# Attention stage of a hybrid encoder layer: the order of three engines' queues written as tables of turns

## The chip, the cores and the metric

The kernel runs on one core of a Trainium2 chip. The metric is the time of one execution on the device, in microseconds. TensorE (PE), VectorE (DVE), ScalarE (ACT), GpSimd (POOL) and SyncE (SP, which issues the transfers) each work through a queue of their own in program order, and wait for each other by semaphores.

## The reference, cut to what matters

One layer with two groups of heads over a prompt of 4096 frames, and a small batch of new frames for eight streams. Mixer A (8 heads) is attention over a window of about 192 keys with a sink per head. Mixer B (8 heads) is attention over 256 chosen keys per query: an indexer scores all admissible keys, the 256 best are kept. For the attention of mixer B the reference reads, cut:

```python
r = relu(einsum('bqhe,ble->bqhl', qi, ki_all))
score = where(adm, einsum('bqhl,bqh->bql', r, wi), -inf)
_, idx = top_k(score, topk)                      # 256 of up to 4096
s = einsum('bqhgd,bqkhd->bqhgk', q, k_all[bi, idx]) * HEAD_DIM ** -0.5
w = softmax(where(valid, s + bias, -inf))
o = einsum('bqhgk,bqkhd->bqhgd', w, v_all[bi, idx])
y = concatenate([oa * silu(ga), ob * silu(gb)]) @ w_out
```

## The kernel before

The program has three stages, one after the other: projections with the indexer and the choice of keys, attention of the prompt (`stage_two`), and the output projection with all of the small batch. The change is in the attention stage alone.

The prompt is cut into 32 tiles of 128 queries. A tile has six jobs: two of mixer A (four heads each, up to 256 keys) and four of mixer B (two heads each, all keys up to the tile's own end, with a mask that is minus a large number where a key was not chosen). A job runs in steps: two for mixer A, one per 512 keys for mixer B, so the number of steps of a tile grows from 8 to 36, and there are 704.

A job's work, engine by engine:

- TensorE `score`: a score unit of up to 512 keys for two heads (L1565, L1576), into one of two PSUM slots.
- VectorE `use`: adds mask or bias, writes the row to SBUF and takes its maximum in parts (L1811 to L1824 for mixer A, L1837 for B); `finish_top` joins the parts (L1850).
- ScalarE `exponential`: in place over the row, 1024 keys at a time (L1673), and the sinks (L1659).
- TensorE `turn`: a step's transposes of the row, four blocks for each of two heads, into one PSUM bank per head (L1592).
- ScalarE (L1771) copies the first head's bank to SBUF, VectorE (L1948) the second head's. The transposes of the next step into a bank wait for its copy.
- TensorE `apply`: the value products of a step from the copies (L1621). The copies are double, so a copy also waits for the products of two steps before.
- The gate: VectorE scales it (L1858 to L1869), TensorE transposes it (`turn_gate`, L1631), ScalarE copies it (L1681), VectorE multiplies (`mix`, L1878).

Two rows of choices, those of tiles 30 and 31, are not ready from the first stage. ScalarE searches their thresholds beside its other work (`late_search`, L1706 and L1688, some 160 turns for each row), and VectorE makes the mask from the result (`late_close`, L1886 to L1929; one of its instructions is a scan over the whole row, L1915).

The order on each engine is written by loops over jobs and steps. On TensorE:

```python
turn(n, g)
for kind, m, j in PLACED[n, g]:
    score(m, j)          # or turn_gate
if last is not None:
    apply(*last)
last = (n, g)
```

So after the transposes of a step come the score units placed at it, and then the value products of the step before. VectorE copies a step, then uses the units placed there; ScalarE copies, then does the exponentials that `PLAN` gives to the step, gate copies, and the late turns that `LATE_ACT` spreads evenly (tiles 3 to 18 and 20 to 28). `LATE_DVE` puts the closing of the late rows into tiles 19 and 29.

Of the kernel before, what the change touches and what calls it, by code (L numbers as in the profile page):

```python
# [128 lines left out]
TESTS = 32  # L129
# [117 lines left out]
""")  # L247

# [1050 lines left out]
LATE_SPANS = {1: ((3, 27, 28),), 2: ((3, 18, 19), (20, 28, 29))}[len(LATE_TILES)]  # L1299


def wide_steps(first, last):

    return [(n, g) for n in range(6 * first, 6 * last + 6) if n % 6 >= 2 for g in range(n_steps(n))]
# [5 lines left out]


LATE_ACT = {_s: 0 for _s in STEP_AT}
LATE_DVE = {_s: 0 for _s in STEP_AT}
for _a, (_first, _last, _close) in zip(LATE_TILES, LATE_SPANS):
    _steps = [(n, g) for n, g in wide_steps(_first, _last) if n % 6 != 5 or g < n_steps(n) - 1]
    _many = TESTS * (len(quarters(_a)) + 1) + 1
    for _i in range(_many):
        LATE_ACT[_steps[_i * len(_steps) // _many]] += 1
    _steps, _many = wide_steps(_close, _close), 2 + 5 * len(quarters(_a)) + 1
    for _i in range(_many):  # L1320
        LATE_DVE[_steps[_i * len(_steps) // _many]] += 1
# [12 lines left out]
def stage_two(nc, rel_bias, sink_a, eye, qk_t, gates, values, chosen, late, ramp, mixed, a_k_prompt, a_v_prompt):  # L1334
    with ExitStack() as ctx:
# [89 lines left out]
        def _(sp):  # L1425
# [121 lines left out]
        def _(pe):  # L1547
# [86 lines left out]
            score(0, 0)  # L1634
            score(1, 0)
            last = None
            for n in range(N_JOBS):
                for g in range(n_steps(n)):
                    turn(n, g)
                    for kind, m, j in PLACED[n, g]:  # L1640
                        if kind == "score":
                            score(m, j)
                        else:
                            turn_gate(m, j)
                    if last is not None:
                        apply(*last)
                    last = (n, g)
            apply(*last)
            turn_gate(TILES - 1, 1)

        @block.scalar
        def _(act):
# [37 lines left out]
            def late_search():  # L1690
# [7 lines left out]
                for i, a in enumerate(LATE_TILES):  # L1698
# [37 lines left out]
                    yield  # L1736
# [23 lines left out]
            late_work = late_search()  # L1760

            for x in PLAN["first"]:
                exponential(*x)
            for n in range(N_JOBS):
                for g in range(n_steps(n)):
                    at = STEP_AT[n, g]
# [5 lines left out]
                    for x in PLAN[n, g]:  # L1772
                        exponential(*x)
                    for kind, m, j in PLACED[n, g]:
                        if kind == "gate":
                            copy_gate(m, j)
                    for _ in range(LATE_ACT[n, g]):
                        next(late_work, None)
            for _ in late_work:
                pass  # L1780
            copy_gate(TILES - 1, 1)

        @block.vector
        def _(dve):
# [17 lines left out]
            def use(n, j):  # L1802
# [5 lines left out]
                if k < 2:  # L1808
                    keys = a_keys(t)
# [14 lines left out]
                    dve.tensor_scalar(top_a[:, k, :], part_a[:, :], -1.0, None, ALU.mult).then_inc(s_top, 1)  # L1824
                    return
                parts = [(i, p) for i, p in enumerate(biased_parts(n)) if c_in(p[0], *score_units(n)[j])]
                for h in range(2):
# [11 lines left out]
                ins.then_inc(s_used, 1)  # L1839
# [4 lines left out]
            def finish_top(n):  # L1844

                k, many = n % 6, len(biased_parts(n))
                dve.wait_ge(s_used, max(UNIT["score", n, j] for j in range(len(score_units(n)))) + 1)
# [32 lines left out]
            def late_close():  # L1880

                over, left, value, low, step, more = (l_pick[:, i:i + 1] for i in range(6))
                for i, a in enumerate(LATE_TILES):
# [31 lines left out]
                    m = tick(dve.tensor_tensor_scan(row, tie, tie, 0.0, ALU.add, ALU.max))  # L1915
                    dve.wait_ge(s_dve, m)
# [6 lines left out]
                    for q, (c, n) in enumerate(parts):  # L1923
                        dve.wait_ge(s_dve, tick.n)
                        tick(dve.scalar_tensor_tensor(late_mask[:, c:c + n], late_tie[:, c:c + n], BIG, late_mask[:, c:c + n], ALU.mult, ALU.add))
                        if q < len(parts) - 1:
                            yield
# [4 lines left out]
            late_work = late_close()  # L1932

            use(0, 0)
            use(1, 0)
            for n in range(N_JOBS):
                t, k = divmod(n, 6)
                if k == 2:
                    scale_gate(t, 0)
                if k == 5:  # L1940
                    scale_gate(t, 1)
                for g in range(n_steps(n)):
                    at = STEP_AT[n, g]
# [5 lines left out]
                    for kind, m, j in PLACED[n, g]:  # L1949
                        if kind == "score":  # L1950
                            use(m, j)
                        else:
                            mix(m, j)
                    for _ in range(LATE_DVE[n, g]):
                        next(late_work, None)
                for m in range(n, min(n + 5, N_JOBS)):
                    if m % 6 >= 2 and job_whose_row(m) == n:
                        finish_top(m)
            mix(TILES - 1, 1)
# [577 lines left out]
```

## Time and profile before

| | us |
|---|---|
| median of three runs | 4878.95 |
| lowest and highest | 4876.77, 4880.1 |
| the profiled execution | 4880.94 |
| its span in the trace | 4879.1 |
| PE busy in the span | 4278.2 (88%) |
| DVE, ACT busy | 3502.0 (72%), 3431.7 (70%) |

Busy shares are means over three stages. The attention stage is the stretch from 2265 us (the first transposes) to 4277 us of the span. Matmuls are pipelined, so the start of one record to the start of the next says more of its cost than its length does.

### The profile page before, as it was taken

Reading aid. Unit: us, or ns where it says so; the run is one execution under the profiler, and the core shown is the slowest. Engines: PE = TensorE matmul, PEld = TensorE weight load, DVE = VectorE, ACT = ScalarE, POOL = GpSimd, SP = SyncE. Lnnn points to the kernel's source line nnn. Section 1 sums busy time; section 2 is a strip of 40 time slices with the busy share of each in tenths; the row PEclk is TensorE's granted clock in tenths of the full one; section 3 lists DMA queues with packets and bytes.
Section 4 is the critical chain, followed back from the end, with each engine's and each line's share of the span. In section 5 each row is a group of like instructions: output and inputs, shape, how many; then the busy total and the mean of one; then the engine's idle time right before and its main releaser. Section 6 shows DMA issues by size and latency. Waiting matters only on the chain. (4 is left out here: it accounts for less than half of the span.)

```text
span 4879.1 us, 78367 instructions
## 1 busy us (share of the span) xinstructions
PE 4278.2 (88%) x26505; PEld 2688.7 (55%) x26505; DVE 3502.0 (72%) x6644; ACT 3431.7 (70%) x6887; POOL 1611.0 (33%) x1358
## 2 busy tenths in 40 slices
PE   7898988778887796763899999999999999989999
PEld 3454444434444343332667777777777777744544
DVE  2478889999999898997777777877677778624111
ACT  1699999999999797932788888688888775510100
POOL 1466667767676777790110000000000000000000
PEclk9999988888898897886999999999999999999999
DMA  6221111111111110014211111010101000055332
GB/s 151 75 73 35 50 40 38 37 36 38 45 48 43 44 43 30 33 70 130 73 55 55 42 41 42 27 57 28 41 24 40 32 25 25 10 162 135 100 101 98
DMA packets 201975, 276.98 MB, mean 57 GB/s; under 512 B 50496, under 2 KB 134176, under 8 KB 201056
## 3 DMA queue, kind: packets, MB, share of 16 engines
q1 hardware_dynamic: 198624, 271.81, 17.7%
q8 instruction: 220, 3.60, 0.3%
q14 instruction: 171, 1.40, 0.1%
q10 hardware_dynamic: 2960, 0.17, 0.0%
HBM read 156.73 MB, written 114.16 MB: 56 GB/s over the span
## 5 line engine op out<-in xcount | busy, mean ns | idle before, releaser
L603 PE MATMUL bank<-w,x 128*128 128x512 f32 (+1 forms) x2848 | 1220.4, 584 | 69.2 <-ACT ring L704 56.3
L1043 DVE TENSOR_SCALAR_CACHE_REDUCE ties<-score,cand 128x512 int8<-128x512 f32 (+13 forms) x448 | 1110.6, 2479 | 82.0 <-POOL score L920 66.2
L603 PEld LDWEIGHTS bank<-w,x 128*128 128x128 f32 x2848 | 551.9, 198 | 645.6 <-issue 525.6
L808 ACT ACTIVATE act_junk<-score,a_cand,a_sign 128x384 int8<-128x384 f32 (+13 forms) x420 | 879.5, 2094 | 14.0
L1837 DVE CUSTOM_DVE_ANT_0 row<-bank,mask 128x512 f32<-128x512 f32 (+3 forms) x1024 | 622.5, 639 | 180.8 <-PE bank L1576 180.1
L1543 POOL TENSOR_TENSOR near_bias<-table,mask 128x2048 f32<-128x2048 f32 (+1 forms) x32 | 129.5, 4048 | 1765.0 <-DVE part L1837 1749.5
L1771 ACT ACTIVATE pT<-bank 128x512 f32<-128x512 f32 (+2 forms) x704 | 368.3, 523 | 427.1 <-PE bank L1592 425.0
L1673 ACT ACTIVATE row<-row,top 128x1024 f32<-128x1024 f32 (+7 forms) x640 | 632.8, 990 | 4.0 <-DVE top L1850 4.0
L1576 PE MATMUL bank<-kT,qb 64*128 64x256 f32 (+1 forms) x4352 | 608.0, 396 | 9.3 <-DVE part L1837 5.9
L1592 PE MATMUL bank<-ident,row 128*128 128x128 f32 x4224 | 593.8, 281 | 25.4 <-DVE pT L1948 19.0
L619 PE MATMUL bank<-kiT,qi 128*128 128x512 f32 (+3 forms) x1136 | 405.3, 493 | 233.8 <-ACT relu L739 233.4
L1948 DVE COPY pT<-bank 128x512 f32<-128x512 f32 (+2 forms) x704 | 425.2, 604 | 255.5 <-PE bank L1592 253.4
L1621 PE MATMUL bank<-pT,v 128*64 128x128 f32 x8448 | 590.3, 280 | 0.0
L915 POOL TENSOR_TENSOR score<-score,relu 128x512 f32<-128x512 f32 (+3 forms) x426 | 553.5, 1299 | 33.4
L1621 PEld LDWEIGHTS bank<-pT,v 128*64 128x64 f32 x8448 | 450.9, 137 | 170.8 <-issue 163.4
L912 POOL TENSOR_TENSOR relu<-relu,weight 128x512 f32<-128x512 f32 (+3 forms) x426 | 500.0, 1174 | 90.7 <-ACT relu L739 90.3
L1592 PEld LDWEIGHTS bank<-ident,row 128*128 128x128 f32 x4224 | 452.8, 141 | 131.2 <-issue 97.5
L2293 PE MATMUL bank<-wo,mix_in 128*128 128x512 f32 x1024 | 451.1, 599 | 0.0
L1576 PEld LDWEIGHTS bank<-kT,qb 64*128 64x128 f32 x4352 | 379.3, 187 | 125.3 <-issue 71.8
L619 PEld LDWEIGHTS bank<-kiT,qi 128*128 128x128 f32 x1136 | 238.0, 225 | 373.5 <-ACT relu L739 291.9
L739 ACT ACTIVATE relu<-bank 128x512 f32<-128x512 f32 (+3 forms) x568 | 292.5, 558 | 119.5 <-POOL score L915 95.0
L2293 PEld LDWEIGHTS bank<-wo,mix_in 128*128 128x128 f32 x1024 | 194.2, 192 | 234.5 <-issue 234.1
(255 smaller groups left out, 4852.5 us busy)
## 6 DMA issues: line engine op xcount, KB each, us to landing
qk_t<-ring SPq DMA_DIRECT2D x66, 256.0 KB, 2.0
gates<-ring SPq DMA_DIRECT2D x66, 256.0 KB, 2.0
gate<-gates SPq DMA_DIRECT2D x33, 512.0 KB, 3.4
out<-x_in SPq DMA_DIRECT2D x33, 512.0 KB, 2.9
x<-in_x_prompt SPq DMA_DIRECT2D x32, 512.0 KB, 3.6
mixed<-mixT SPq DMA_DIRECT2D x64, 256.0 KB, 2.0
mix_in<-mixed SPq DMA_DIRECT2D x32, 512.0 KB, 4.2
x_in<-in_x_prompt SPq DMA_DIRECT2D x32, 512.0 KB, 3.9
```

Source lines behind the costliest of these rows:

```text
L603: ins = pe.matmul(p_bank[n % 2][:, 0:n1 - n0], held[:, c * P:(c + 1) * P], w[:, c, n0:n1], start=(c == 0), stop=(c == KC - 1))
L619: ins = pe.matmul(s_bank[at % 4][:, 0:n], qi[:, part, h * P:(h + 1) * P], kiT[:, c:c + n], start=(part == 0), stop=(part == 1))
L808: tick(act.activation(junk, row, ACT.Sign, bias=c, scale=back, accum_out=a_sum[:, :]))
L912: k = tick(pool.tensor_tensor(r, r, weighs, ALU.mult))
L915: pool.tensor_tensor(to, to, r, ALU.add).then_inc(s_pa, 1)
L1043: n = tick(dve.tensor_scalar(ties[:, 0:width], row, c.bitcast(F32), 0.0, ALU.is_ge, ALU.add, accum_out=counts[:, i:i + 1]))
L1576: ins = pe.matmul(s[:, h * STEP + c0:h * STEP + c0 + m], qb[t % 2][half, g, :], kT[half, c + c0:c + c0 + m], start=True, stop=True)
L1592: ins = pe.transpose(t_bank[h][:, b * P:(b + 1) * P], held, ident[:, :])
L1621: ins = pe.matmul(oT[0 if k < 2 else 1][half * HD:(half + 1) * HD, col:col + P], value, pT[h][at % 2][:, b * P:(b + 1) * P], start=first, ...
L1673: act.activation(at, at, ACT.Exp, bias=bias, accum_out=out).then_inc(s_exp, 1)
L1837: ins = dve.tensor_tensor_reduce(row[k % 2][:, h, c0:c0 + w0], s[:, h * STEP + c0 - c:h * STEP + c0 - c + w0], more, 1.0, PAD, ALU.add, AL ...
L2293: ins = pe.matmul(y_bank[k % 2], held, w[:, c, i * STEP:(i + 1) * STEP], start=(c == 0), stop=(c == KC - 1))
```

## The change

Each of the three engines' orders becomes a table, as a string of letters with counts; a generator per kind of work yields after each item, and `take_turns`, which is there already for the first stage, takes the next item of the kind that the table names. Each kind keeps its own order. TensorE has transposes of one head (`t`), score units and gates (`u`) and value products of a step (`v`); ScalarE has copies (`p`), exponentials (`e`), gate copies (`g`) and late turns (`l`); VectorE has copies (`p`), joined maxima (`t`), pieces of units and mixes (`u`), gate scalings (`k`) and late closing (`l`). The even spreads of late work are gone. A score unit's pieces on VectorE are separate turns; since the table may now put them before work that the loops had put first, `use` and `finish_top` wait for the maximum before and for the transposes that read the old row. SP loads the second late row at tile 19 instead of 20. `PLACED` and `PLAN` still give the sequence within a kind.

```diff
+PE_TURNS_2 = in_turn("""
+u2 t6 u2 v2 t2 v2 t3 v t v u5 t3 u t v t u t v t u t2 v2 t2 v t3 v t2 v2 u4 t2 u t u t v t v t u t u t v t2 v t v t2
...
+ACT_TURNS_2 = in_turn("""
+e3 p e4 p e9 p2 e3 p e p g e4 p2 e4 p e4 p e2 g e5 p e2 p e3 p2 l6 g l2 e3 p e l p l e3 p e6 p g e6 p e2 p e3 p l g l
...
+DVE_TURNS_2 = in_turn("""
+u2 p4 u3 t u t p2 k u3 t u2 t u p u2 p t k u p u2 p u t u p4 k u3 t u2 t u p u k p u3 t u p u2 p u3 p t k p2 u3 p u3 t
...
-                if t in [close + 1 for _, _, close in LATE_SPANS[:-1]]:
-                    load_late([close + 1 for _, _, close in LATE_SPANS].index(t) + 1)
+                if t in LATE_LOADS:
+                    load_late(LATE_LOADS.index(t) + 1)
...
                         ins = pe.transpose(t_bank[h][:, b * P:(b + 1) * P], held, ident[:, :])
                     ins.then_inc(s_t0 if h == 0 else s_t1, 1)
+                    yield
...
+            def applies():
+                for n, g in STEP_AT:
+                    apply(n, g)
+                    yield
+
+            take_turns(PE_TURNS_2, t=turns(), u=units(), v=applies())
...
+            take_turns(ACT_TURNS_2, p=copies(), e=exponentials(), g=gate_copies(), l=late_search())
...
                 if k < 2:
+                    dve.wait_ge(s_top, TOP_AT[n])
+                    if t:
+                        dve.wait_ge(s_t1, STEP_AT[n - 6, n_steps(n - 6) - 1] + 1)
...
+                if t:
+                    before = job_whose_row(n)
+                    dve.wait_ge(s_top, TOP_AT[before] + 1)
+                    dve.wait_ge(s_t1, STEP_AT[before, min(j, n_steps(before) - 1)] + 1)
...
-                ins.then_inc(s_used, 1)
+                        if h == 1 and (i, (c0, w0, near)) == parts[-1]:
+                            ins.then_inc(s_used, 1)
+                        yield
...
+            take_turns(DVE_TURNS_2, p=copies(), t=tops(), u=uses(), k=gates_scaled(), l=late_close())
```

`take_turns`, unchanged:

```python
def take_turns(order, **work):
    for kind, many in order:
        for _ in range(many):
            next(work[kind])
```

## Rows read from the trace of the kernel before

**Rows 1.** Windows: stretch, us, busy of PE, PEld, DVE, ACT, POOL (instructions), clock.

```profile
2264.99:2831.61 566.62, 524.64 (x5008) 385.33 (x5008) 420.84 (x1276) 459.52 (x1219) 61.27 (x15) 0.97 0.21 65
2831.61:3257.46 425.85, 405.06 (x4043) 307.06 (x4041) 322.38 (x873) 332.61 (x771) 24.90 (x6) 0.98 0.13 42
3257.46:4277.38 1019.92, 1006.34 (x10242) 771.04 (x10240) 726.97 (x1929) 759.11 (x1634) 41.23 (x10) 1.00 0.09 29
```

**Rows 2.** Who waited for whom in the attention stage: us in total, times, longest us.

```profile
PE bank L1592 <- DVE pT L1948: 32.6, 31, 8.2
...
PE bank L1592 <- ACT pT L1771: 26.5, 73, 1.8
...
PE bank L1592 <- ACT row_a L1673: 13.1, 1, 13.1
```

**Rows 3.** Timeline of TensorE in tile 19: start us, us, line, operation, records.

```profile
3100.19 0.66 PE L1592 MATMUL bank<-ident,row_a 128*128 128x128 f32 x4 [0.26 <-ACT pT L1771]
3100.77 0.66 PE L1621 MATMUL bank<-pT,va 128*64 128x128 f32 x8
...
3103.67 0.66 PE L1621 MATMUL bank<-pT,va 128*64 128x128 f32 x8
3104.26 1.09 PE L1592 MATMUL bank<-ident,row 128*128 128x128 f32 x8
3105.29 1.13 PE L1576 MATMUL bank<-kT,qb 64*128 64x256 f32 x8
3106.35 1.09 PE L1621 MATMUL bank<-pT,v 128*64 128x128 f32 x16
3107.38 1.09 PE L1592 MATMUL bank<-ident,row 128*128 128x128 f32 x8
...
3113.60 1.09 PE L1592 MATMUL bank<-ident,row 128*128 128x128 f32 x8
3114.53 0.60 PE L1631 MATMUL bank<-ident,scaled 128*128 128x128 f32 x4
```

**Rows 4.** Timeline of TensorE in tile 22: two score units in a row.

```profile
3408.16 1.13 PE L1565 MATMUL bank<-ka,qa 64*128 64x256 f32 x8
3409.13 1.03 PE L1576 MATMUL bank<-kT,qb 64*128 64x256 f32 x8
3410.09 1.09 PE L1621 MATMUL bank<-pT,v 128*64 128x128 f32 x16
```

**Rows 5.** Timeline of all engines, tile 25: transposes and their two copies.

```profile
3600.82 1.09 PE L1592 MATMUL bank<-ident,row 128*128 128x128 f32 x8
...
3601.52 0.60 ACT L1771 ACTIVATE pT<-bank 128x512 f32<-128x512 f32 x1 [0.87 <-PE bank L1592]
...
3601.95 0.69 DVE L1948 COPY pT<-bank 128x512 f32<-128x512 f32 x1 [0.59 <-PE bank L1592]
```

**Rows 6.** Timeline of all engines, tile 23: a copy, and transposes waiting for it.

```profile
3421.68 0.38 ACT L1771 ACTIVATE pT<-bank 128x256 f32<-128x256 f32 x1
...
3422.12 0.66 PE L1592 MATMUL bank<-ident,row_a 128*128 128x128 f32 x4 [0.26 <-ACT pT L1771]
```

**Rows 7.** Windows for lines L1706 and L1688 alone: stretch, us, ACT busy (instructions).

```profile
2264.99:4277.38 2012.39, 334.56 (x512) 0.99 0.13 42
...
2264.99:4277.38 2012.39, 70.01 (x294) 0.99 0.13 42
```

**Rows 8.** View by windows, tiles 20 to 24.

```profile
3178.50:3589.14 410.64, 404.24 (x4095) 307.95 (x4094) 292.89 (x819) 336.71 (x746) 20.42 (x5) 1.00 0.12 39
```

**Rows 9.** Groups by form on DVE: count, busy us, mean ns, idle before.

```profile
L1837 DVE DVE_READ_ACCUMULATOR2_ANT part<- 128x1 f32 x1336 | 110.8, 83 | 0.0
```

**Rows 10.** View by windows of tile 19; waits of TensorE in tile 19, then in tile 29.

```profile
3094.77:3178.50 83.73, 73.23 (x718) 55.99 (x716) 77.13 (x174) 44.46 (x105) 4.46 (x1) 0.94 0.10 31
...
PE bank L1592 <- DVE pT L1948: 9.8, 3, 8.2
...
PE bank L1592 <- DVE pT L1948: 6.1, 3, 5.4
```

More of the change, by code:

```diff
@@ new lines @@
+t v2 u2 t3 v u t2 u v2 u t4 u t2 v2 u2 t2 v2 t2 u t2 u t2 v2 u t2 u t2 v2 u2 t2 v u t2 v u t2 v u t2 u t2 v2 u t2 u
+t2 v2 u2 t2 v2 u2 t4 v2 u t2 u t2 v u t2 v t2 v2 t4 u t2 v2 u2 t2 v2 t2 u t2 v2 u2 t2 u t2 u t2 v2 u2 t2 v2 t2 u t2
+v2 u2 t4 v u t2 u v2 u t4 v u t2 u2 t v2 u t4 v u t2 u t v2 u2 t2 v2 t2 u t2 v u2 t2 v u t2 u t2 v2 u2 t2 v2 t2 u t2
+v2 t4 v t2 v u t2 u t2 v2 u2 t2 v2 t2 u t2 v u2 t2 u t2 v2 u2 t2 v2 u t4 v u t2 u t2 v2 u2 t2 v2 t2 u t2 v u t2 u2 t
+v2 u t4 v2 u2 t4 v2 u2 t2 u t2 u t v2 u2 t2 v2 u2 t4 v u t2 v2 u2 t2 u t2 v t2 v2 t4 u t2 v2 u2 t2 v2 t2 u t2 v2 u2
@@ new lines @@
+t4 u t2 v2 u2 t2 v2 t2 u t2 v2 u2 t4 v u2 t2 u t2 v2 u2 t2 v2 u t4 v u t2 u t2 v2 u t2 v2 t4 v2 t4 v2 t4 v2 t2 u t2
+v2 t4 v2 t4 v2 t4 v2 t4 v2
+""")
+ACT_TURNS_2 = in_turn("""
+e3 p e4 p e9 p2 e3 p e p g e4 p2 e4 p e4 p e2 g e5 p e2 p e3 p2 l6 g l2 e3 p e l p l e3 p e6 p g e6 p e2 p e3 p l g l
+p l2 e3 p e l p e7 p e3 l p g e3 p e4 p e3 p l g l p l2 e4 p l p e5 p e5 l p l e3 p e g e3 p e3 p g l p l2 p l p e2 p
+e2 l p l2 p l p l e9 p e p g e5 p e4 p e g l p l p l3 p e p e l e p e p l3 p e2 p e7 p e p l g l e6 p e2 p e p e g p
@@ new lines @@
+e3 p2 e2 p4 e3 p e3 p e4 p e4 p e4 p e4 p3 e g e p e2 p e p e2 p e p5 g p3 e2 p e2 p e2 p e2 p5 e2 p e3 p e3 p3 e2 p3
+e2 p e4 p e4 p e4 p e4 p e4 p2 g p e p e2 p e p e p e p e2 p5 g p2 e3 p e2 p e2 p e p4 e2 p e2 p e2 p e2 p2 e2 p3 e2
+p e2 p e6 p e2 p e2 p e5 p e3 p2 g p e p e2 p e p e2 p e p e p4 g p3 e3 p e3 p e2 p5 e p e p e2 p e p e2 p e p2 g p9
+""")
+DVE_TURNS_2 = in_turn("""
+u2 p4 u3 t u t p2 k u3 t u2 t u p u2 p t k u p u2 p t u p4 k u3 t u2 t u p u k p u3 t u p u2 p u3 p t k p2 u3 p u3 t
@@ L247 @@
+u2 l u p u l2 p u2 p u2 l4 p u2 p u2 l3 p u p u3 l t l2 p u2 p u2 p u2 k p u2 p u p u4 p u p u5 t p u2 p u2 p u2 p u3
+p u2 p u2 p u2 p u4 k p t u p4 u2 p u2 p u4 p2 u2 p u2 p u3 p u4 t p u4 p2 u2 p u2 p u2 p u2 p u2 p u4 t u2 p2 u2 p
+u2 p u2 k u p u2 p u2 p u5 p u t p u2 p u2 p u2 p u3 p u2 p u2 p u2 p u4 k t u p5 u2 p u4 p2 u2 p u2 p u2 p u2 p u5 t
+p u4 p2 u2 p u2 p u2 p u4 p2 u4 t p6 k p10 u
 """)
@@ L1298 @@
 QUARTER = 1024
-LATE_SPANS = {1: ((3, 27, 28),), 2: ((3, 18, 19), (20, 28, 29))}[len(LATE_TILES)]
-def wide_steps(first, last):
-    return [(n, g) for n in range(6 * first, 6 * last + 6) if n % 6 >= 2 for g in range(n_steps(n))]
+LATE_LOADS = (19,)
 def quarters(a):
     return [(c, min(QUARTER, (a + 1) * P - c)) for c in range(0, (a + 1) * P, QUARTER)]
[L1312 to L1321, printed above, removed]
 def exps_of_job(n):
@@ L1632, in turn_gate, with turns, units @@
                 ins.then_inc(s_unit, 1)
[L1634 to L1649, printed above, removed]
+            def turns():
+                for n, g in STEP_AT:
+                    yield from turn(n, g)
+            def units():
+                for kind, n, j in UNIT:
+                    if kind == "score":
+                        score(n, j)
+                    else:
+                        turn_gate(n, j)
+                    yield
+            def applies():
+                for n, g in STEP_AT:
+                    apply(n, g)
+                    yield
+            take_turns(PE_TURNS_2, t=turns(), u=units(), v=applies())
         @block.scalar
@@ L1758, in late_search, with copies @@
                     yield
[L1760 to L1766, printed above, removed]
+            def copies():
+                for (n, g), at in STEP_AT.items():
                     act.wait_ge(s_t0, at + 1)
@@ L1771, in _, with exponentials, gate_copies @@
                     act.activation(pT[0][at % 2][:, 0:cols], t_bank[0][:, 0:cols], ACT.Copy).then_inc(s_c0, 1)
-                    for x in PLAN[n, g]:
+                    yield
+            def exponentials():
+                for s in ["first"] + list(STEP_AT):
+                    for x in PLAN[s]:
                         exponential(*x)
[L1774 to L1781, printed above, removed]
+                        yield
+            def gate_copies():
+                for kind, t, b in UNIT:
+                    if kind == "gate":
+                        copy_gate(t, b)
+                        yield
+            take_turns(ACT_TURNS_2, p=copies(), e=exponentials(), g=gate_copies(), l=late_search())
         @block.vector
@@ L1915, in late_close @@
                     m = tick(dve.tensor_tensor_scan(row, tie, tie, 0.0, ALU.add, ALU.max))
+                    yield
                     dve.wait_ge(s_dve, m)
@@ L1930, in late_close, with copies @@
                     yield
[L1932 to L1943, printed above, removed]
+            def copies():
+                for (n, g), at in STEP_AT.items():
                     dve.wait_ge(s_t1, at + 1)
@@ L1948, in _, with tops, uses, gates_scaled @@
                     dve.tensor_copy(pT[1][at % 2][:, 0:cols], t_bank[1][:, 0:cols]).then_inc(s_c1, 1)
[L1949 to L1959, printed above, removed]
+                    yield
+            def tops():
+                for n in TOP_AT:
+                    if n % 6 >= 2:
+                        finish_top(n)
+                        yield
+            def uses():
+                for kind, n, j in UNIT:
+                    if kind == "score":
+                        yield from use(n, j)
+                    else:
+                        mix(n, j)
+                        yield
+            def gates_scaled():
+                for t in range(TILES):
+                    for b in range(2):
+                        scale_gate(t, b)
+                        yield
+            take_turns(DVE_TURNS_2, p=copies(), t=tops(), u=uses(), k=gates_scaled(), l=late_close())
 NEW = BATCHES * DEC
```

81 lines of the change are left out of this document (78 added, 3 removed).

## The prediction

> **What bounds the kernel now.** I read the profile by stretches of the attention stage, cut where the first transposes of tiles 0, 15 and 21 start; it takes 2012 us of the 4879 [rows 1]. Tensor is busy in 525 of 567, 405 of 426 and 1006 of 1020 us, so the later the tile the more it alone sets the pace; its idle time is 42.0 + 20.8 + 13.6 = 76.4 us. Scalar has 107, 93 and 261 us free, vector 146, 103 and 293. Next the waits of tensor [rows 2]: 32.6 us for vector's copies of transposed blocks, 26.5 us for scalar's, and 13.1 us once at the start, for the first exponentials. That is all that an order can remove as idle time.
>
> Busy time is not all work. In the timeline of tensor [rows 3] a step in the middle of a tile goes round without a gap in 3.12 us: 8 transposes 1.03 (3104.26 to 3105.29), one score unit 1.06, 16 value records 1.03. The 4 transposes of a mixer-A step take 0.58 to the next start and the 8 of a mixer-B step 1.03, so one costs 0.11, and each visit to the transposes has a fee of 1.03 - 0.88, some 0.14. Value products: 0.59 for two blocks (3103.67), 1.03 for four, so 0.22 a block and a fee of 0.15. Where 8 transposes are followed by the gate's transposes the next start comes after 0.93 (3113.60 to 3114.53): the part of the fee that is paid on leaving is 0.09, on entering 0.05. Two score units in a row [rows 4] take 1.93 (3408.16 to 3410.09), so the second adds 0.87 and the fee of a visit is 0.19. With the order of the loop, tensor makes 705 visits to transposes (the gate's among them), 563 to scores, 703 to value products: 98.7 + 107.0 + 105.5 = 311 us of fees. A reordering can thus change tensor's busy time, not only its waits.
>
> **What the change does, part by part.** No matrix, vector or scalar operation is added or dropped; the orders on tensor, scalar and vector are replaced by tables. I counted the tables against the loops.
>
> *Fewer visits.* The new tensor table has 626 visits to transposes, 491 to scores, 431 to value products. Saved: 79 x 0.14 + 72 x 0.19 + 272 x 0.15 = 11.1 + 13.7 + 40.8 = 65.5 us; by stretch 14.7, 12.6, 38.2. The trace before has no two value products in a row that show a merged visit, nor scores followed by transposes; a merged value visit saves between 0 and 0.15. I take 0.15, since the merged score units and the transposes before the gate's both save the whole fee. With 0 the savings would be 24.8 us.
>
> The Trainium skill, TensorEngine Tiling (Array Packing), Key Properties, says that changing the tiling mode, not just the tile, drains TensorE. The three kinds here have shapes 128*128, 64*128 and 128*64, and the rows agree in that transposes after transposes pay no fee. By it merged value products save all of their 40.8 us, as taken.
>
> *Transposes with nothing between.* In the loop at least one value product or unit stands between the transposes of a step and those of the next. In the table 215 steps have nothing there. The transposes of the next step write the same bank, so they wait for the copy. From [rows 5]: transposes start at 3600.82, scalar's copy of the first head starts 0.70 later and takes 0.60, and tensor resumes 0.06 after a copy's end (3421.68 + 0.38 to 3422.12, [rows 6]): 1.36. Tensor comes to the next transposes after 0.05 + 8 x 0.11 = 0.93. So it stands 0.43 us at each place where both heads come right before; there are 114 (30, 21 and 63 by stretch): 49.0 us. The second head follows vector's copy, ready 1.13 + 0.69 + 0.06 = 1.88 after the start, against 1.36 + 0.44: 0.08 more in the 81 of them where it follows at once, 6.5 us. In the other 101 the first head of the step had gone earlier; in 42 of these the second head follows directly and waits for vector's copy, 1.39 - 0.93 = 0.46: 19.3 us. Together 74.9 us (19.7, 14.4 and 40.8), with copies that start at once. If the copies come late it is more; where another engine holds tensor up anyway it is less, down to half.
>
> *Waits of the old order.* Of the 76.4 us, 13.1 belong to the start and stay. The two long waits for vector, 8.2 us in tile 19 and 5.4 in tile 29 [rows 10], stand where the loop puts vector's closing of a late row, whose scan is one instruction in both kernels; the table moves the first close to tiles 14 and 15 and leaves the scan of the second in tile 29, so I let both stay. Of the other 49.7 us, most stand before transposes of mixer A, where the loop has one value product alone between two steps; the table has 45 such places instead of 110 (the bare ones are charged above). None to all may come back; I take half, 24.9 us.
>
> *Late search on scalar.* It was spread evenly over tiles 3 to 18 and 20 to 28. The table packs it: 160 turns in tiles 0 to 14 (101 before), 22 in tiles 15 to 20 (77), 138 after (144). A turn is (334.6 + 70.0) / 322 = 1.26 us [rows 7]. In the first stretch scalar goes from 459.5 to 534 of 567 us; with the 13.1 at the start 547 is its floor, and my forecast for the stretch is 566.6 - 14.7 + 19.7 - 14.5 = 557. In tiles 20 to 24 there are 142 turns for 83: 336.7 + 59 x 1.26 = 411 us, in a time that is now 410.6 [rows 8]. So those tiles cannot become faster, whatever tensor saves. Tensor's own account there is near even too, so I add nothing; the bound above is the rival.
>
> *Vector's units in pieces, more waits.* A unit's pieces become single turns, so a copy can go between two of them. New waits on maxima and on the second head's transposes come to some 1,400; each stands in front of its unit, and copies queue behind it. No row shows a wait's own price; between nothing and the shortest vector row, 0.083 us [rows 9], that is 0 to 116 us, beside vector's 542 free ones [rows 1]. I take nothing; without that cover it would be slower by as much as lies on the path. The load of the second late row is asked for one tile earlier on SP; its wait for the first mask is over by then (closed in tile 15), so the loads queued behind it are not held.
>
> **Sum.** -65.5 + 74.9 - 24.9 = -15.5 us on the profiled execution's 4880.94, that is 4865.4. That execution is 2.0 above the median of the runs, 4878.95, so I predict 4863. The last stage follows attention on tensor, so what is gained there counts in full.
>
> **The rivals.**
> 1. *Scalar is crowded, slower.* The place is tiles 0 to 14 and 20 to 24, 302 turns of late search. One that stands ahead of a copy that tensor is about to need costs up to its 1.26 us. For it: scalar has no free time left in tiles 20 to 24. Against: turns are placed where the tables leave scalar nothing else. With one turn in eight, 38 x 1.26 = 48 us, and the result is 4911. It decides from about one in fifteen: 25 us, which ends above the median.
> 2. *Much faster.* The fees go as worked out, half of the bare waits fall together with waits that are there anyway (37 us), and all 49.7 us come back: -65.5 + 37.5 - 49.7 = -78, 4801. For it: 29 of the old waits are in the first stretch, where mixer A has much of the work. Against: in tiles 21 to 31, where tensor has 98.7% already, savings (38.2) and bare waits (40.8) cancel.
> 3. *No change.* Fees and bare waits cancel, and what of the old waits comes back is spent on late copies: within 10 us of 4879. This is the case in which the change doesn't do what it says: the tables give tensor's priorities, but it runs its queue in order and waits where the table has nothing to put in.
> 4. *The clock.* After the 8.2 us wait the granted clock of tile 19 is 0.94 [rows 10], so 83.7 x 0.06 = 5 us of full clock were lost; in tiles 20 to 24 it is 1.00. If many short stops did the same in ten tiles, 50 us: 4913. The stops here are 0.43 us, a stop of 0.26 at 3422.12 [rows 6] lies in tiles at 1.00, and so do the other short ones there, so I give it little. The Trainium skill, TensorE: Matmul & The Clock Gate, A second HAM failure mode, describes such falls from frequent short idling between groups of matmuls; the trace of before does not show one.
>
> **How the numbers follow.** Forecast 0.37 (4845 to 4872), much faster 0.18, no change 0.18, scalar crowded 0.24, clock 0.03. A difference under 0.2%, 10 us, is about what a measurement of this kernel can't tell from none: faster means under 4869, slower over 4889. The forecast lies nearly all under 4869, so faster 0.52, same 0.20 (no change and the forecast's upper edge), slower 0.28 (the two slow rivals and a little of no change). The range goes to 4815 (most of rival 2's way, its bottom left out) and 4908 (most of rival 1): 0.08 and 0.12 stay outside. The forecast's own range is 4845 to 4872.
>
> **What the profile after would show.** Value products, scores and transposes with a lower busy sum, some 60 us less of tensor's busy time in the attention stage, against more idle time: waits before transposes for scalar's and vector's copies near 100 us where they were 59, in many short pieces of 0.4. Scalar over 95% busy in tiles 20 to 24, and around 60% after tile 25. Tensor's waits in tile 19 gone and 8 us in tile 15. I am wrong on the fees if busy time stays; on the bare waits if idle time stays near 76; and if tensor waits for scalar's exponentials or copies by 0.5 to 1.3 us at a time in tiles 20 to 24, it is rival 1.

## The result, and the profile after

After: 4890.61 us, median of 12 runs (4886.7 to 4897.69), against 4878.93 for the kernel before in the same rounds. The ratio is 1.0025 (95% interval 1.0016 to 1.0033): slower by 0.25%, where I forecast 4863 and faster. The time lies inside the range, the direction was wrong. One run of a later experiment (84 places filled) took 5427.57 us at a granted clock of 0.78 instead of 0.93 and is left out of its median.

The loss is in the attention stage: 2025.9 us instead of 2012.4 in the profiled executions. What lies outside it, where the two kernels are alike, was 6.2 us shorter there, so the two spans differ by 7.3 us only. By windows (stretch, us, busy of PE, PEld, DVE, ACT, POOL, clock), the three stretches of [rows 1], then tile 19 [rows 10] and tiles 20 to 24 [rows 8]:

```profile
2262.20:2831.73 569.53, 514.46 (x4993) 388.06 (x4994) 425.62 (x1294) 526.88 (x1371) 61.31 (x15) 0.97 0.20 65
2831.73:3251.72 419.99, 400.35 (x4071) 310.75 (x4069) 305.17 (x860) 275.54 (x646) 24.54 (x6) 0.99 0.13 42
3251.72:4288.10 1036.38, 989.03 (x10230) 776.94 (x10228) 703.12 (x1924) 748.32 (x1607) 41.74 (x10) 1.00 0.09 29
3098.30:3168.60 70.30, 69.22 (x714) 54.13 (x713) 49.51 (x144) 43.31 (x98) 4.10 (x1) 1.00 0.19 67
3168.60:3588.91 420.31, 400.30 (x4118) 311.64 (x4116) 281.78 (x817) 403.54 (x890) 20.44 (x5) 1.00 0.10 33
```

TensorE is busy for 1903.8 us instead of 1936.0, yet idle for 122.1 instead of 76.4. The stretches came out 2.9 slower, 5.8 faster and 16.5 slower. Tile 19 got 13.4 faster, since the closing of a late row left it (it now stands in tiles 14 and 15, which got 15.5 slower together); tiles 20 to 24 got 9.7 slower, with ACT busy for 96%.

The waits of TensorE in the attention stage (us in total, times, longest), answering to [rows 2]:

```profile
PE bank L1678 <- ACT pT L1854: 44.9, 90, 1.6
PE bank L1678 <- DVE pT L2037: 40.2, 48, 6.2
PE bank L1678 <- ACT row_a L1762: 16.6, 7, 13.4
PE bank L1708 <- DVE pT L2037: 10.5, 9, 6.9
...
PE bank L1708 <- ACT pT L1854: 4.4, 12, 0.6
```

L1678 is the transposes, L1708 the value products. Transposes wait for copies for 85.1 us where it was 59.1. New is that value products wait too, 14.9 us.

What joining visits gives shows in TensorE's timeline of tile 25:

```profile
3645.47 1.09 PE L1678 MATMUL bank<-ident,row 128*128 128x128 f32 x8
3646.49 1.97 PE L1708 MATMUL bank<-pT,v 128*64 128x128 f32 x32
3648.39 2.00 PE L1662 MATMUL bank<-kT,qb 64*128 64x256 f32 x16
3650.32 1.09 PE L1678 MATMUL bank<-ident,row 128*128 128x128 f32 x8
```

Two steps' value products take 1.90 (3646.49 to 3648.39) where two visits took 2 x 1.03 [rows 3]; two units take 1.93. The fees are gone as worked out.

A place where the transposes of a step follow directly on those of the step before is called bare from here on; there are 215. TensorE can go on there only when the bank that it is about to write again has been copied. A bare place whose copy starts at once, which is called a prompt copy below (tile 31; a bracket gives the idle time before and what ended it):

```profile
4274.73 1.09 PE L1678 MATMUL bank<-ident,row 128*128 128x128 f32 x8
4275.43 0.60 ACT L1854 ACTIVATE pT<-bank 128x512 f32<-128x512 f32 x1 [2.49 <-PE bank L1678]
...
4276.08 1.19 PE L1678 MATMUL bank<-ident,row 128*128 128x128 f32 x8 [0.25 <-ACT pT L1854]
```

From start to start 1.35 us, forecast 1.36. And one whose copy does not (tile 22):

```profile
3346.22 1.09 PE L1678 MATMUL bank<-ident,row 128*128 128x128 f32 x8
...
3347.58 0.39 ACT L1777 ACTIVATE l_cand<-l_sign,l_cand,l_step 128x1 f32<-128x1 f32 x1
3347.87 0.58 ACT L1854 ACTIVATE pT<-bank 128x512 f32<-128x512 f32 x1
...
3348.50 1.09 PE L1678 MATMUL bank<-ident,row 128*128 128x128 f32 x8 [1.20 <-ACT pT L1854]
```

Here ACT is in a late turn until 3347.87, and such a place costs 2.28 us.

To split the difference I went through TensorE's records item by item. An item's price is the least time from its start to the next one's start that occurs for the same kinds of neighbours; what an item takes beyond it is a wait. Price and waits are counted from the first score units on, some 15 us ahead of tile 0, so their sum is larger than the attention stage.

| kernel | visits: transposes, units, products | price | waits | attention |
|---|---|---|---|---|
| before | 705, 563, 703 | 1892 | 134 | 2012 |
| after | 626, 491, 431 | 1840 | 199 | 2026 |
| 115 bare places made in before | 590, 563, 703 | 1886 | 228 | 2100 |
| 178 joined units in before | 705, 385, 703 | 1856 | 167 | 2009 |
| 141 chosen pairs in before | 705, 422, 596 | 1849 | 137 | 1972 |
| after, 84 bare places filled | 709, 491, 513 | 1856 | 180 | 2024 |
| after, 177 products moved | 776, 491, 571 | 1873 | 205 | 2065 |
| own tables | 723, 427, 599 | 1852 | 94 | 1933 |

So the tables save 51 us of fees and add 65 us of waits. The split depends on how finely neighbours are told apart: finer and coarser classes give 45 to 60 us saved and 58 to 74 added, always some 14 us apart.

### The profile page after: what moved, and what is told of

It is laid out like the page before. It is cut to its first block and busy times, and to the rows that moved or that the text cites. A ratio compares the mean times of both kernels' runs of the same rounds, so it can differ in the third digit from the quotient of the medians.

```text
span 4886.4 us, 79007 instructions
## 1 busy us (share of the span) xinstructions
PE 4242.2 (87%) x26505; PEld 2698.8 (55%) x26505; DVE 3465.8 (71%) x6644; ACT 3431.1 (70%) x6887; POOL 1612.1 (33%) x1358
## 5 line engine op out<-in xcount | busy, mean ns | idle before, releaser
L1678 PE MATMUL bank<-ident,row 128*128 128x128 f32 x4224 | 604.9, 282 | 78.6 <-ACT pT L1854 41.6
L1933 DVE CUSTOM_DVE_ANT_0 row<-bank,mask 128x512 f32<-128x512 f32 (+3 forms) x1024 | 620.3, 635 | 37.8 <-PE bank L1662 15.9
L1662 PE MATMUL bank<-kT,qb 64*128 64x256 f32 (+1 forms) x4352 | 584.0, 394 | 10.0 <-DVE mixT L1977 7.8
L1678 PEld LDWEIGHTS bank<-ident,row 128*128 128x128 f32 x4224 | 454.7, 141 | 247.5 <-issue 123.4
L1708 PE MATMUL bank<-pT,v 128*64 128x128 f32 x8448 | 550.6, 279 | 3.4 <-DVE pT L2037 1.3
L1708 PEld LDWEIGHTS bank<-pT,v 128*64 128x64 f32 x8448 | 458.0, 137 | 74.8 <-issue 69.4
```

The costliest lines, as they stand in the source:

```text
L1662: ins = pe.matmul(s[:, h * STEP + c0:h * STEP + c0 + m], qb[t % 2][half, g, :], kT[half, c + c0:c + c0 + m], start=True, stop=True)
L1708: ins = pe.matmul(oT[0 if k < 2 else 1][half * HD:(half + 1) * HD, col:col + P], value, pT[h][at % 2][:, b * P:(b + 1) * P], start=first, ...
L1933: ins = dve.tensor_tensor_reduce(row[k % 2][:, h, c0:c0 + w0], s[:, h * STEP + c0 - c:h * STEP + c0 - c + w0], more, 1.0, PAD, ALU.add, AL ...
```

## The experiments

Theory 1 was that the fees are real and that bare places and late copies ate them; the rivals were that ACT and DVE set the pace, the added DVE waits, and the late work.

**Bare places filled (177 products moved).** In the changed kernel:

```diff
+def filled(order):
+    out, halves = [], 0
+    for kind in [kind for kind, many in order for _ in range(many)]:
+        if kind == "t":
+            halves += 1
+            if halves % 2 and halves > 1 and out[-1] == "t":
+                k = len(out) - 2
+                k -= out[k] == "t"
+                while k > 0 and out[k] not in "tv":
+                    k -= 1
+                if out[k] == "v":
+                    out.append(out.pop(k))
+        out.append(kind)
+    return [(kind, 1) for kind in out]
...
-            take_turns(PE_TURNS_2, t=turns(), u=units(), v=applies())
+            take_turns(filled(PE_TURNS_2), t=turns(), u=units(), v=applies())
```

> The changed kernel with one thing altered: wherever transposes of a step directly follow transposes of the step before, the nearest value product that stands ahead of them is moved in between; that fills 177 places and leaves 38. ACT and DVE keep the changed tables. Theory 1 (bare places cost more than forecast, since copies are late): the 97 us that TensorE waits in bare places after the change falls by about four fifths (-80), some 140 value-product visits come back at 0.15 (+21), 150 transposes' visits at about 0.04 net (+5): about -54 us, near 4836. Theory 2 (ACT and DVE set the pace, waits of TensorE only move): no gain, the fees come on top, 4890 to 4920. Theory 3 (the added waits on DVE made it slower): as theory 2, within 4890 to 4916.

Measured 4931.52, 1.0105 of before (1.0091 to 1.0119), 41 us above the changed kernel. Theory 1 failed outright. The rule moved 177 products, but it took some of them out of a place that it had filled just before: 157 places end up filled and 58 stay bare, not 38. The price rose by 33 us and the waits did not fall. In 34 places the wait was now for a copy that itself waited for the value product just put in front (copies are double): 27.5 us. Units waited more for their slots (2.0 and 7.8 us in the changed kernel):

```profile
PE bank L1679 <- DVE part L1950: 14.2, 27, 2.5
PE bank L1679 <- DVE mixT L1994: 10.6, 11, 6.0
```

**Filled only where that cannot happen (84).** The same function, but only between two whole steps and only with the product of the step before:

```diff
-            if halves % 2 and halves > 1 and out[-1] == "t":
-                k = len(out) - 2
-                k -= out[k] == "t"
+            if halves % 2 and halves > 1 and out[-2:] == ["t", "t"]:
+                k = len(out) - 3
...
-                if out[k] == "v":
+                if out[k] == "v" and halves // 2 - out[:k].count("v") == 2:
```

> The changed kernel, filled in 84 places only: those where the step's two transposes stand together and the value product moved in between is that of the step before (which the waiting copy does not itself wait for; in the run with 177 filled places 31 waits were for a copy that waited for the very product moved in between). Theory 1 (a bare place costs its copy's whole time, more than the visits it saves): 84 x 0.38 to 0.5 us of waits go (-32 to -42), 84 value-product and transposes' visits come at 0.15 + 0.09 (+20): -12 to -22 us, 4869 to 4878. Theory 2 (a bare place costs about what it saves, the loss is elsewhere): within 6 us of 4890.

Measured 4889.92, 1.0021 of before (1.0012 to 1.003): the changed kernel's time to within a microsecond. Theory 2 holds. In 29 of these places the copy had been prompt; the 0.36 us wait went and a fee of 0.15 to 0.2 came. In most of the others the wait stayed: of 55 places where ScalarE was still at something else when the transposes ended, 44 wait in this kernel too, and 29.9 of 41.8 us are left. The place of tile 22 shown above, in this kernel:

```profile
3342.73 0.93 PE L1694 MATMUL bank<-ident,row 128*128 128x128 f32 x7
3343.59 1.09 PE L1724 MATMUL bank<-pT,v 128*64 128x128 f32 x16
...
3345.00 0.57 ACT L1870 ACTIVATE pT<-bank 128x512 f32<-128x512 f32 x1
...
3345.62 1.09 PE L1694 MATMUL bank<-ident,row 128*128 128x128 f32 x8 [0.94 <-ACT pT L1870]
```

TensorE now does 1.03 us of work in the gap and still waits 0.94. The work is not new: the product stood ahead of the transposes, so these now start earlier against ACT's queue. ACT's copy starts 2.44 us after them (the first starts at 3342.56, just outside the view), where it was 1.65. At such places the next transposes come when ACT's queue reaches the copy, and not sooner for work moved on TensorE.

**Bare places in the loops.**

```diff
+                two = u != s and u[0] == s[0] and s[0] % 6 >= 2 and s[0] >= 6 * 8 and plain(s) and plain(u)
+                seen += two
+                if two and seen % 2 == 0:
+                    turn(*s)
+                    turn(*u)
+                    place(s)
+                    apply(*last)
+                    place(u)
+                    apply(*s)
```

> The kernel before, where in 89 of 178 pairs of steps of a wide job (tiles 8 to 31, every second pair) the second step's transposes are moved up directly behind the first's: 89 bare places are made and 89 visits to transposes saved, nothing else. Theory 1: each costs the wait for a copy, 0.4 to 0.6 us in the changed kernel's bare places, less about 0.04 net of a visit: +32 to +50 us, 4911 to 4929. Theory 2 (TensorE's waits are slack of other engines, so a wait made here is given back at the next one): less than +10 us.

Measured 4963.15, 1.0171 (1.0157 to 1.0185): +83.9 us. The rule made 115 pairs, not 89 (after a pair that is passed over, its second step may begin the next), so 0.73 us each, above theory 1's price. Of 80 us of waits in these places, 91 that wait for a prompt copy on ACT have 33 (0.36 each); the 16 behind DVE's gate scalings and the late closing have 18, and 19 behind late turns on ACT have 19. The price fell by only 5.7 us, 0.05 per merged visit to the transposes. Theory 2 is out here: in the loops' order nothing gives such a wait back.

**Score units joined.**

```diff
+                if two:
+                    turn(*s)
+                    place(s)
+                    place(u)
+                    apply(*last)
+                    turn(*u)
+                    apply(*s)
```

> The kernel before, where in 178 pairs of steps of a wide job (tiles 8 to 31) the second step's score unit is moved up directly behind the first's, ahead of the value product: transposes, two units, value product, transposes, value product. That saves 178 visits to score units and makes no bare place. Theory 1 (a visit's fee is real and gained in full where no wait comes in its place): 178 x 0.19 = -34 us, near 4845. Theory 2 (other engines set the pace): 0 to +10, since TensorE then only waits longer for copies and units' banks.

Measured 4874.01, 0.9988 (0.9979 to 0.9997). The price fell by 35.5 us, 0.20 for each of 178 visits: theory 1's fee, which made 34. The waits rose by 32.4. Two kinds grew, those for units' slots (5.9 us in 9 waits before) and those for ScalarE's copies (26.5 in 73):

```profile
PE bank L1576 <- DVE part L1854: 14.9, 38, 1.6
PE bank L1592 <- ACT pT L1788: 40.0, 93, 2.3
```

The second unit of a pair comes while DVE still uses the slot. The time, 5 us below before, lies between the theories and near theory 2 (0 to +10), while the fee is theory 1's.

**Pairs chosen.** Units joined in 141 pairs (all in tiles 8 to 31), the value products too in 107 of them, in the places where by the traces' durations neither a copy nor a slot comes late.

```diff
+                turn(*s)
+                place(s)
+                if i in SPLIT or i in WHOLE:
+                    u = steps[i + 1]
+                    place(u)
+                    if i in WHOLE:
+                        turn(*u)
+                    apply(*last)
+                    if i in SPLIT:
+                        turn(*u)
+                    apply(*s)
```

> The kernel before with 141 pairs of steps of a wide job joined (tiles 5 to 31), chosen so that by the durations in the traces neither a copy nor a unit's bank comes late: both score units stand together in all of them (141 x 0.20 = -28 us by the prices of the run with 178 pairs), and in 107 the two value products as well (107 x 0.15 = -16 us). DVE and ACT keep the loops of before. Theory 1 (a saved visit is gained where no copy or bank comes late in its place): -44 us, near 4835. Theory 2 (ACT and DVE set the pace, so most is given back as waits, as in the run with 178 pairs, which kept 5 of 35): -6 us, near 4873.

Measured 4835.57, 0.9911 (0.9897 to 0.9924): -42 us, theory 1, and faster than both kernels. The stretches:

```profile
2262.98:2824.84 561.86, 519.22 (x5008) 387.25 (x5008) 418.22 (x1276) 457.93 (x1219) 61.29 (x15) 0.97 0.21 65
2824.84:3243.03 418.19, 396.27 (x4042) 309.44 (x4041) 318.95 (x873) 329.85 (x771) 24.88 (x6) 0.99 0.13 42
3243.03:4235.19 992.16, 977.38 (x10242) 780.19 (x10240) 713.49 (x1930) 750.38 (x1634) 41.22 (x10) 1.00 0.09 30
```

27.8 us come from tiles 21 to 31. A pair in tile 22:

```profile
3331.93 1.09 PE L1603 MATMUL bank<-ident,row 128*128 128x128 f32 x8
3332.96 2.00 PE L1587 MATMUL bank<-kT,qb 64*128 64x256 f32 x16
3334.89 1.09 PE L1603 MATMUL bank<-ident,row 128*128 128x128 f32 x8
3335.91 1.97 PE L1632 MATMUL bank<-pT,v 128*64 128x128 f32 x32
```

Transposes, two units, transposes, two steps of products: about 1.9 us lies between any transposes and the next. ACT's copies start later here than in the changed kernel (in the median 0.51 us after their transposes end, against 0.32), and TensorE hardly waits more for them than in the kernel before (28.1 us in 79 waits, against 26.5 in 73).

**The added DVE waits alone**, in the kernel before:

```diff
+                    dve.wait_ge(s_top, TOP_AT[n])
+                    if t:
+                        dve.wait_ge(s_t1, STEP_AT[n - 6, n_steps(n - 6) - 1] + 1)
...
+                    dve.wait_ge(s_top, TOP_AT[before] + 1)
+                    dve.wait_ge(s_t1, STEP_AT[before, min(j, n_steps(before) - 1)] + 1)
...
+                dve.wait_ge(s_top, TOP_AT[n])
```

> The kernel before, its loops untouched, with only the change's additional DVE waits (on the row maximum and the transposes of the job that held the row buffer, ahead of each use of a score unit, and one ahead of each row maximum; 640 semaphore instructions). Theories 1 and 2: the waits are met long before and DVE has slack, so within 4 us of 4879. Theory 3 (these waits are what made the change slower): +8 to +15 us, 4887 to 4894.

Measured 4880.09, 1.0001 (0.9993 to 1.001). Theory 3 is out; the waits cost nothing measurable, as taken. (They are some 1,400 waits, which take 640 instructions more.)

**Late work made light**, the same edit in both kernels:

```diff
-                    edge = float(width - 2 * TOPK + 1)
+                    edge = 0.0
...
-                            late_tick(act.activation(late_junk[:, 0:n], late_row[:, c0:c0 + n], ACT.Sign, bias=c, scale=scale,
+                            late_tick(act.activation(late_junk[:, 0:64], late_row[:, c0:c0 + 64], ACT.Sign, bias=c, scale=scale,
...
-                    row, tie = late_row[:, 0:width], late_tie[:, 0:width]
+                    row, tie = late_row[:, 0:64], late_tie[:, 0:64]
```

> The changed kernel with the late tiles' search made light: its 256 sweeps on ACT read 64 columns in place of about 1024 and the two scans on DVE 64 in place of about 4000 (so the masks of tiles 30 and 31 are no longer those of the reference). All waits, tables and orders stay. By the trace, late work ahead of a copy cost TensorE 47 us after the change and 20 before. Theory 1 (late work that the tables put ahead of copies ate part of the gain): the changed kernel gains about 45 to 50 us, the kernel before with the same edit about 20, so it ends 10 to 20 us below that. Theory 2 (bare places and their prompt copies alone): both gain alike and the changed kernel stays 8 to 15 us above.

> The kernel before with the same light late search (sweeps of 64 columns on ACT, scans of 64 on DVE; the masks of tiles 30 and 31 are not those of the reference). Theory 1: late work ahead of copies costs 20 us here, so 4855 to 4862, above the changed kernel with the same edit. Theory 2: it gains as much as the changed kernel does and stays below it by 8 to 15 us.

Measured 4863.05, 0.9963 of before (0.9951 to 0.9976), and 4850.33, 0.9939 (0.9926 to 0.9951). Both gain alike, 27.6 and 27.4 us, and the changed kernel stays 12.7 above. Theory 1 expected the reverse. The sweeps and scans cost the two kernels the same in total, so their length is not the difference. The edit leaves the rest of the late work where it stood: against the kernel before with the same edit, the changed one is still 7.4 us slower in tiles 20 to 24 and 9.6 in tile 29, where VectorE closes the second late row.

**One exponential later.** In the changed kernel's ACT table, 38 copies that had made TensorE wait changed places with the exponential before them:

```diff
+        if kind == "p":
+            if copies in EARLIER:
+                out[-2:] = ["p", out[-2]]
+            copies += 1
```

> The changed kernel with 38 copies of ACT's table moved ahead of the one exponential that stands before them: those behind which, by its trace, TensorE waited (24.7 us in all) while ACT was still at that exponential. Theory 1 (ACT's order makes copies late and that is where the gain went): -12 to -25 us, 4866 to 4878. Theory 2 (the exponential set back is needed as soon as the copy was, or ACT then waits for the transposes): within 6 us of 4890, or above.

Measured 4898.83, 1.0038 (1.0025 to 1.005), 6 to 8 us above the changed kernel (1.0025, 1.0016 to 1.0033), so no gain. Waits behind exponentials fell from 34 to 22 us, waits for copies that were prompt rose from 31 to 40, waits behind late turns from 47 to 52, those for units' slots from 18 to 23. Theory 2: what the earlier copies gave came back as other waits.

**Each half alone.** The tables up to tile 19 and the loops' order from tile 20 (shown), and the reverse, with SP's load at tile 20 again:

```diff
+TO = STEP_AT[6 * 20, 0]
+PE_TURNS_3 = joined(PE_TURNS_2, "t", 2 * TO, PE_LOOP)
+ACT_TURNS_3 = joined(ACT_TURNS_2, "p", TO, ACT_LOOP)
+DVE_TURNS_3 = joined(DVE_TURNS_2, "p", TO, DVE_LOOP)
```

> The changed kernel's three tables up to the end of tile 19 (late work of the first late tile included), and from tile 20 on the order of the loops before (the second late tile's work spread as before). Theory 1 (each stretch keeps its own sum: by the two traces tiles 0 to 14 cost 2.9 us more and tiles 15 to 19 9.9 less, and the loss of 20 us sits in tiles 20 to 31): about 7 us below the kernel before, 4868 to 4876. Theory 2 (the loss is carried over: what the tables leave behind at the end of a stretch is paid later, wherever they end): 4879 to 4890.

> The other half of the run with the tables up to tile 19: here the order of the loops up to the end of tile 19 (first late tile's work spread as before) and the changed kernel's three tables from tile 20 on. Theory 1 (the loss sits in tiles 20 to 31, by the two traces +4.1 in tile 20 and +16.5 in tiles 21 to 31): 20 us above the kernel before, 4896 to 4904. Theory 2 (part of it is carried in from the first half's tables): 4880 to 4892.

Measured 4871.5, 0.998 (0.9971 to 0.9989), and 4900.42, 1.0039 (1.0025 to 1.0053). Windows of tiles 0 to 19 and 20 to 31, with the tables in the first half, then in the second:

```profile
2264.05:3172.22 908.17, 838.74 (x8285) 640.61 (x8285) 676.52 (x1990) 730.88 (x1853) 81.85 (x20) 0.98 0.18 57
3172.22:4270.73 1098.51, 1082.16 (x11006) 828.39 (x11004) 781.91 (x2090) 820.56 (x1768) 45.31 (x11) 1.00 0.09 29
```

```profile
2261.96:3180.39 918.43, 857.37 (x8285) 636.94 (x8285) 691.14 (x1996) 729.74 (x1853) 82.08 (x20) 0.98 0.17 54
3180.39:4299.58 1119.19, 1067.30 (x11006) 836.60 (x11004) 756.62 (x2082) 819.82 (x1769) 45.84 (x11) 0.99 0.09 31
```

The same halves took 913.5 and 1098.9 in the kernel before, 906.4 and 1119.5 in the changed one. Each keeps its own sum to a few us, and nothing is carried over: the whole loss, 20 us, is made in tiles 20 to 31. It is not spread evenly there: by the two traces tiles 20 to 24 are 9.7 us slower, tile 29 is 7.4 slower, tile 31 is 4.3 slower, and tiles 25 to 28 take the same 380 us.

**Own tables.** The chosen pairs, and single turns moved by one or two where a wait goes (three tables of the same kind, not shown):

```diff
 PE_TURNS_2 = in_turn("""
...
 ACT_TURNS_2 = in_turn("""
...
 DVE_TURNS_2 = in_turn("""
...
-LATE_LOADS = (19,)
+LATE_LOADS = (20,)
```

> The changed kernel's machinery with three other tables: the order with 141 joined pairs, in which single turns (a value product, a score unit, a copy on ACT or DVE, a part of the late search) are moved one or two turns where the durations in the traces say that a wait goes; no transposes are put directly behind those of the step before. Visits: units 427, value products 599, transposes 723 (563, 703 and 705 before). Theory 1 (fees and waits are both TensorE's own, gained where no new wait comes): fees 136 x 0.20 + 104 x 0.15 = -43 us, and of the 134 us of waits some 40 to 60 go: 4775 to 4800. Theory 2 (below some point ACT and DVE set the pace and waits come back): 4815 to 4840, no better than the joined pairs alone.

Measured 4797.8, 0.9829 (0.9816 to 0.9842): theory 1, -83 us, the fastest of all. By the table above 40 us are fees and 40 us are waits. Stretches, and what is left of the waits for copies:

```profile
2261.09:2802.61 541.52, 514.83 (x5008) 385.35 (x5008) 419.43 (x1277) 458.13 (x1221) 61.29 (x15) 0.98 0.22 68
2802.61:3213.10 410.49, 395.33 (x4043) 310.21 (x4041) 319.64 (x874) 329.12 (x769) 24.90 (x6) 0.98 0.13 43
3213.10:4193.71 980.61, 974.11 (x10242) 780.03 (x10240) 713.24 (x1929) 750.77 (x1633) 41.22 (x10) 1.00 0.09 30
```

```profile
PE bank L1686 <- DVE pT L2045: 25.7, 16, 8.5
...
PE bank L1686 <- ACT pT L1862: 10.3, 17, 2.7
```

## Why the prediction was wrong, step by step

Against its sum, -65.5 + 74.9 - 24.9 = -15.5, the traces give -51 + 97 - 62 + 20 + 10 = +14 or so for the attention stage. Three steps failed: the fee of the transposes (14 us short), the bare places "with copies that start at once" (22 us short), and the waits of value products, which stood nowhere in the sum (20 us). The term for the old waits was wrong by 37 us the other way, so that the time came out only 28 us off is partly luck.

- *Fewer visits.* Value products saved 39.8 of 40.8, units 11.4 of 13.7; the sizes 0.15 and 0.19 were right, as the joined units and the chosen pairs confirm. Transposes saved nothing, where 11.1 were forecast. I charged the net number of visits. In truth 215 are merged and 136 made, 127 of them by splitting a step's two heads and the rest around the gate's transposes. Transposes of a step that follow those of the step before still pay 0.05 (0.49 us from start to start for four blocks of 0.11, also where nothing is waited for), so a merge of two whole steps saves 0.05, and a split costs 0.15. The sentence in the prediction that transposes after transposes pay no fee is wrong by that 0.05. Short by 14 us.
- *Bare places.* The price of a prompt one was right, 1.35 against 1.36 from start to start. But only 69 of the 156 waits in bare places were for a copy that started at once, 27 us; some 66 us stood behind something else on the copy's engine: exponentials 25, late work 30 (17 behind ScalarE's search, 12 behind VectorE's closing), gate work and units 10 (the last few were for exponentials themselves). In the loops a copy was due every 3.1 us, and an exponential of 1.1 us fits between two of them. Merged transposes come 1.35 us apart and then not for a while, and an exponential that stands between their copies makes the second one late. 97 instead of 75. This I had named ("if the copies come late it is more") and left at nothing.
- *Value products.* Not in the sum at all: taken last and together, they come soon after their own copies. 25 us of waits, where it was 6.
- *Old waits.* 62 came back, not 25: mixer A's places with one value product alone are nearly gone. I took half where all was right. The 62 hold the two long waits in tiles 19 and 29, 14 us, that I had let stay. They did not vanish: behind VectorE's copies in tiles 14, 15 and 29 TensorE now waits 25.6 us (part of the bare places and value products above), where it was 15.9 in tiles 19 and 29 [rows 10]. In tile 29:

```profile
PE bank L1678 <- DVE pT L2037: 13.0, 7, 6.2
```

- Short waits below 0.06 us each grew by about 10 in sum.

*The rivals.* The nearest was "no change", which has the mechanism: tensor's queue waits where the table has nothing to put in, and what comes back is spent on late copies; the time ended 2 us outside its band of 10 us. "Scalar is crowded" was right in part. ACT is busy for 403.5 us in tiles 20 to 24 (forecast 411), and its sign is there: 11 waits of 0.5 to 1.3 us for ACT's copies and 3 longer ones, where the kernel before has one over 0.5. But bare waits behind ScalarE's late turns are 17 us in all, 8 of them in tiles 20 to 24, not 48, and with the search made light those tiles are still 7.4 us slower. "The clock" is out: the granted clock was 1.00 in tiles 21 to 31 with over 60 short stops, and 0.99 in that stretch of the loops with bare places. The Trainium skill, TensorE: Matmul & The Clock Gate, A second HAM failure mode, tells of a kernel where frequent short idling between groups of matmuls made the clock swing; these traces show no such thing in that stretch.

*Signs named beforehand.* Waits before transposes for copies "near 100": 85.1; with the value products' 14.9, which the sign did not name, 100.0. Busy time "some 60 us less": 32. The fees saved are 51, and since the modelled ends of records cover part of the waits, 65 us of added waits show as 45.7 us of idle time. ACT over 95% in tiles 20 to 24: 96%; around 60% after tile 25: 60% from there on. Tile 19's long wait gone: yes, and 6.9 us in tile 15 (forecast 8).

What stays open is why ACT, at 72% in tiles 21 to 31, is behind at just those places. Moving 38 copies ahead of one exponential each did not help. A place to look is what ACT itself waits for, since its queue runs in order too (whole attention stage, changed kernel):

```profile
ACT pT L1854 <- PE bank L1708: 117.2, 60, 9.9
ACT row L1762 <- DVE top L1949: 48.3, 39, 3.2
ACT row_a L1762 <- DVE top_a L1915: 22.9, 21, 2.5
```

The first line is copies that wait for value products, which is not found in the kernel before; the other two are exponentials that wait for VectorE's maxima, 71.2 us where it was 12.5. So much of ACT's free time lies in front of work that is not ready, and a copy that stands behind that work has to wait as well. No run shows that this is the cause: the own tables, the fastest, have 166.3 us of the first kind, but only 10.4 of the second. A PE order of the changed kernel with a freely rebuilt ACT order was not tried.

## What to carry to other kernels

Joining like items on TensorE pays when other work stays between each item and the one that needs its result from another engine: 141 joined pairs chosen for that gave 42 us, 178 pairs not chosen gave 5, and 215 merged visits to transposes with nothing between saved at most 0.05 us each and brought 97 us of waits. Price a merge by the pair of neighbours that it makes, not by visits counted, and price the place that it empties by how late the other engine's queue may be, not by the bare duration of the copy. When a gap is filled with work moved from just before it and keeps its wait, the other engine sets the pace there.

## What the runs showed that I had not expected

That filling a gap with 1 us of real work, moved from just ahead of it, left the wait nearly as long (1.20 us without, 0.94 with it), and that 640 more semaphore instructions on a DVE busy for 72% cost nothing measurable (1.0001, 0.9993 to 1.001).
